# The entry of a two-block transformer kernel: modulation products shared between two engines, x normed by parts, two output groups run together

## The reference

```python
c_act = silu(c)                              # c: 2048 values
mod = c_act @ w_ada + b_ada                  # w_ada: 2048 x 12288
sh1, sc1, gt1, sh2, sc2, gt2 = split(mod, 6)
h = rmsnorm(x, g_mix) * (1 + sc1) + sh1
proj = h @ w_in                              # w_in: 2048 x 11344
q_a, k_a, v_a, q_b, k_b, v_b, qi, ki, wi, g_a, g_b = split(proj, ...)
...
x = x + (1 + gt1) * mixer(h, ...)
```

## Time and profile before

| | us |
|---|---|
| median of 3 runs (lowest, highest) | 2721.91 (2721.4, 2722.2) |
| the profiled execution's own time | 2720.93 |
| span of the profile, first to last instruction | 2719.1 |
| PE busy in the span | 2598.8 (96%) |
| DVE busy in the span | 1949.7 (72%) |
| ACT busy in the span | 1217.5 (45%) |

### The profile page before, as it was taken

One profiled execution on the slowest core, in us unless ns is written; L12 is line 12 of the kernel. 1 busy time (PEld: TensorE's weight loads), 2 busy tenths in 40 slices (PEclk: granted clock), 3 DMA queues, 4 the chain that ended last, 5 costly groups with the idle time before them and its releaser, 6 DMA issues.

```text
span 2719.1 us, 39494 instructions
## 1 busy us (share of the span) xinstructions
PE 2598.8 (96%) x14637; PEld 2265.9 (83%) x14637; DVE 1949.7 (72%) x2761; ACT 1217.5 (45%) x1578; POOL 101.5 (4%) x145
## 2 busy tenths in 40 slices
PE   3499999999999999999999999998999999999998
PEld 3388888888887888888888888886888888888887
DVE  6986778887788988855666656998776645566554
ACT  1244653444554655544555552003554443444443
POOL 0011111100001000000000000000000000000000
PEclk8599999999999999999999999999999999999999
DMA  8898677875678677755666554552556655666553
GB/s 312 308 291 274 210 241 241 252 213 155 218 249 269 209 248 248 242 186 188 187 190 187 190 166 141 154 155 78 192 180 187 191 187 191 188 187 191 186 186 132
DMA packets 492581, 557.33 MB, mean 205 GB/s; under 512 B 18855, under 2 KB 458280, under 8 KB 492200
## 3 DMA queue, kind: packets, MB, share of 16 engines
q1 hardware_dynamic: 474023, 488.50, 56.1%
q0 software_dynamic: 18432, 67.12, 8.2%
HBM read 553.45 MB, written 2.10 MB: 204 GB/s over the span
## 4 chain that ended last, share of the span: by engine, by line
PE 92%; DVE 4%; issue 2%; DMA 1%; ACT 1%; SPq 1%; POOL 0%; DVEq 0%; ACTq 0%
PE ps L1467 53%; PE ps L1469 26%; PE ps L1757 8%; DVE wlo L865 1%; PE ms L1520 1%; DVE norm_rows L962 1%; PE ms L1498 1%; DMA att<-in_w_ada 1%; PE ms L1782 1%; DMA att<-in_x 0%; PE ms L1611 0%; DVE tCDE L962 0%; SPq L396 0%; PE ms L1767 0%; PE ms L1545 0%
## 5 line engine op out<-in xcount | busy, mean ns | idle before, releaser
L865 DVE TENSOR_TENSOR wlo<-raw,whi 128x1024 fp32r<-128x1024 f32 x794 | 971.0, 1224 | 619.7 <-ACT whi L522 609.9
L1467 PE MATMUL ps<-xhl,whi 128*128 128x512 f32 x4352 | 1381.9, 399 | 23.0 <-DVE xhl L926 16.7
L522 ACT CAST whi<-raw 128x1024 fp32r<-128x1024 f32 x794 | 831.4, 1050 | 1126.6 <-PE ps L1469 1045.4
L1469 PEld LDWEIGHTS ps<-xhl,wlo 128*128 128x128 f32 x4352 | 821.0, 189 | 193.9
L1469 PE MATMUL ps<-xhl,wlo 128*128 128x256 f32 x4352 | 858.6, 279 | 0.0
L1467 PEld LDWEIGHTS ps<-xhl,whi 128*128 128x128 f32 x4352 | 666.8, 190 | 33.2 <-issue 32.7
L1467 PE MATMUL ps<-ghl,whi 128*128 128x512 f32 x1024 | 319.7, 393 | 0.0
L1469 PEld LDWEIGHTS ps<-ghl,wlo 128*128 128x128 f32 x1024 | 192.3, 188 | 44.3
L1757 PE MATMUL ps<-xg,raw 128*128 128x256 f32 x1024 | 221.3, 379 | 0.0
L1467 PE MATMUL ps<-fhl,whi 128*128 128x512 f32 x704 | 219.3, 393 | 0.0
L1757 PEld LDWEIGHTS ps<-xg,raw 128*128 128x128 f32 x1024 | 194.7, 190 | 26.2
(11 more groups left out here) (245 smaller groups left out, 1500.3 us busy)
## 6 DMA issues: line engine op xcount, KB each, us to landing
raw<-in_w_in SPq DMA_DIRECT2D x176, 512.0 KB, 4.3
raw<-in_w_up SPq DMA_DIRECT2D x176, 512.0 KB, 4.2
ada<-in_w_ada POOLq DMA_DIRECT2D x128, 512.0 KB, 4.7
raw<-in_ffn_w_up SPq DMA_DIRECT2D x128, 512.0 KB, 3.7
raw<-in_ffn_w_down SPq DMA_DIRECT2D x128, 512.0 KB, 3.4
raw<-in_conv_w_pw SPq DMA_DIRECT2D x96, 512.0 KB, 3.6
raw<-in_w_down SPq DMA_DIRECT2D x88, 512.0 KB, 3.3
att<-in_w_ada SPq DMA_DIRECT2D x32, 1024.0 KB, 7.3
```

The costliest lines, as they stand in the source:

```text
L522: nc.scalar.copy(whi[t % SPL][:, :, :], raw[t % RAW][:, :, :]).then_inc(s_hi, 1)
L865: nc.vector.tensor_tensor(wlo[t % SPL][:, :, :], raw[t % RAW][:, :, :], whi[t % SPL][:, :, :].bitcast(F32), ALU.subtract).then_inc(s_lo, 1)
L1467: mm(o[:, m, :, :], whi[t % SPL][:, c, m * P:(m + 1) * P], x, start=first and c == 0, stop=last and c == KC - 1, skip_group_check=True)
L1469: ins = mm(o[:, m, 0, :], wlo[t % SPL][:, c, m * P:(m + 1) * P], x[:, 0, :], start=False, stop=last and c == KC - 1, skip_group_check=True)
```

## The change

For the first eight modulation groups, which are now taken in the order 0, 4, 1, 5, 2, 6, 3, 7 (a shift group and its scale group make a pair, `FIRST`):

- Quarter 0 of K (`BY_TENSOR` = 4 chunks) is no longer multiplied by DVE. PE loads each 128x128 block of w_ada as weights and multiplies it by one column of `cact` (`first_columns`, 16 one-column products a group), into the same PSUM column to which `first_modulation` then adds DVE's two sums. This quarter has two buffers, the others one each.
- DVE makes the other 12 products and, between its first four and its last eight, other work (`beside`): reading out the group before, the root in group 2, norming four chunks of x in groups 2, 4 and 6 (`norm_first`), two wlo in groups 3, 5 and 7.
- Output groups 0 and 1 are multiplied together through K, as units 0 to 7 (`EARLY`): an even unit goes to `ps[0]`, an odd one to `ps[1]`, both with the same four chunks of x. A pair of units stands in groups 3, 5 and 7 between `first_columns` and `first_modulation`, the last pair after group 7. SP loads the pairs behind groups 1, 3, 5 and 6.
- `c` moves up in the list of vectors; SP loads the identity and the first 128 rows of vectors first, then w_ada and x, then the rest. ACT copies the two other blocks of vectors.
- The rotary angles and sines move out of the entry into `background` of steps 5 to 13.
- The main loop starts at t = 5 (unit 8), and the half pieces follow a new schedule (`pieces_by`): none in steps 0 to 2, two in steps 4, 7 and 10, otherwise one. POOL's first two are sent for at the end of the seventh group.

```diff
+BY_TENSOR = 4
+BY_VECTOR = DC - BY_TENSOR
+EARLY = 8
+B_ANGLE = 5
 
...
+def pieces_by(s):
+
+    return max(0, s - 2) + (s >= 4) + (s >= 7) + (s >= 10)
+
...
 
-VECS = [("b_ada", 96), ("g_mix", 16), ("g_ffn", 16), ("conv_b", 88), ("conv_w", 264), ("g_final", 16),
+VECS = [("b_ada", 96), ("c", 16), ("g_mix", 16), ("g_ffn", 16), ("conv_b", 88), ("conv_w", 264), ("g_final", 16),
         ("norm_mix_g_2", 16), ("norm_ffn_g_2", 16), ("final_norm_g_2", 16), ("conv_b_pw1_2", 32),
         ("conv_w_dw_2", 16 * TAPS), ("conv_b_dw_2", 16), ("conv_ln_g_2", 16), ("conv_ln_b_2", 16),
-        ("conv_b_pw2_2", 16), ("c", 16)]
+        ("conv_b_pw2_2", 16)]
 AT, _n = {}, 0
 for _name, _rows in VECS:
...
 
-        ada_first = [att[:, 32 + 8 * q:40 + 8 * q, :].rearrange("p (c m) t -> p c (m t)", c=4) for q in range(4)]
+        ada_first = [att[:, 32 + 8 * q:40 + 8 * q, :].rearrange("p (c m) t -> p c (m t)", c=4) for q in range(5)]
...
 
-        first_sum = [mod_sum, [tCDE[:, 0:NCOL], tCDE[:, NCOL:2 * NCOL]]]
...
+        first_vecs = [v for v in vec_parts if v[3] < P]
+        other_vecs = [v for v in vec_parts if v[3] >= P]
...
+            sp.dma_start(cons[:, 0:C_SW128], A["consts"][:, 0:C_SW128]).then_inc(s_in[0], 16)
+            load_vectors(sp, first_vecs, s_vin[0])
...
-            for q in range(4):
-                sp.dma_start(ada_first[q][:, :, :], w_ada[q][:, :, 0:NCOL]).then_inc(s_adaring[q], 16)
-            x_in = A["x"].rearrange("b (c p) (h t) -> p (b c) h t", p=P, t=T)
-            for c in range(2):
-                sp.dma_start(att[:, 8 * c:8 * c + 8, :], x_in[:, c]).then_inc(s_in[2], 16)
-            with sp.Fori(1, ADA_START) as g:
-                for q in range(4):
-                    sp.wait_ge(s_chain, g * DC + 4 * (q + 1))
-                    sp.dma_start(ada_first[q][:, :, :], w_ada[q][:, :, bass.ds(g * NCOL, NCOL)]).then_inc(s_adaring[q], 16)
+            def first_quarter(n, q):
+
+                cols_at = slice(FIRST[n] * NCOL, (FIRST[n] + 1) * NCOL)
+                if q == 0:
+                    if n >= 2:
+                        sp.wait_ge(s_firstmm, n - 1)
+                    sp.dma_start(ada_q0[n % 2][:, :, :], w_ada[0][:, :, cols_at]).then_inc(s_adaq0[n % 2], 16)
+                else:
+                    if n:
+                        sp.wait_ge(s_first, BY_VECTOR * (n - 1) + 4 * q)
+                    sp.dma_start(ada_first[q][:, :, :], w_ada[q][:, :, cols_at]).then_inc(s_adaring[q], 16)
...
-            columns(0, 28, w_in, 0)
+            for q in (1, 2, 3):
+                first_quarter(0, q)
+            x_in = A["x"].rearrange("b (c p) (h t) -> p (b c) h t", p=P, t=T)
+            for c in range(2):
+                sp.dma_start(att[:, 8 * c:8 * c + 8, :], x_in[:, c]).then_inc(s_in[2], 16)
+            first_quarter(0, 0)
+            sp.dma_start(posi, A["positions"]).then_inc(s_in[1], 16)
+            load_vectors(sp, other_vecs, s_vin[1])
+            sp.dma_start(cons[:, C_SW128:], A["consts"][:, C_SW128:]).then_inc(s_rest, 16)
+            for n in range(1, ADA_START):
+                for q in range(4):
+                    first_quarter(n, q)
+                if n in (1, 3, 5, 6):
+                    quad = {1: 0, 3: 1, 5: 2, 6: 3}[n]
+                    for k in range(2):
+                        load(0, 2 * quad + k, w_in[quad][:, :, CW * k:CW * (k + 1)])
+            columns(EARLY, 26, w_in, 2 * CW)
...
-                pool.wait_ge(s_chain, DC * (1 + ADA_START) + 2 * max(0, m - 1))
+                if m < 2:
+                    pool.wait_ge(s_first, BY_VECTOR * (ADA_START - 1))
+                else:
+                    pool.wait_ge(s_chain, DC * (1 + ADA_START) + 2 * (m - 1))
...
-            act.wait_ge(s_trc, 3)
+            act.wait_ge(s_trc, 1)
...
+                act.wait_ge(s_tr, 9 + b + 1)
+                lo = P + 4 * P * b
+                nc.scalar.copy(cols[:, lo:lo + 4 * P], (bank_z, bank_f)[(9 + b) % 2]).then_inc(s_trc, 1)
...
-            act.wait_ge(s_ang, 1)
-            for n in range(2):
-                nc.scalar.activation(rope[:, 2 * n, :], rB[:, T * n:T * (n + 1)], ACT.Sin).then_inc(s_sin, 1)
-                nc.scalar.activation(rope[:, 2 * n + 1, :], rA[:, T * n:T * (n + 1)], ACT.Sin).then_inc(s_sin, 1)
-            for t in range(SPL):
-                split_hi(0, t)
+            def first_hi(j):
+
+                for c in range(4 * j, 4 * j + 4):
+                    act.wait_ge(s_nt, c + 1)
+                    nc.scalar.activation(xh[:, c, :], sq[:, c % 4, :], ACT.Identity, bias=mod[:, c:c + 1]).then_inc(s_nh, 1)
+
             root(0)
-            norm_hi(0, lambda c: mod[:, c:c + 1])
+            for j in range(4):
+                first_hi(j)
+                split_hi(0, 2 * j)
+                split_hi(0, 2 * j + 1)
...
+                if s == B_ANGLE + 5:
+                    act.wait_ge(s_ang, 1)
...
-            for t in range(1, T_WAB + 1):
+            for t in range(EARLY - 3, T_WAB + 1):
                 split_hi(0, t + 3)
+                if t == EARLY - 1:
+                    low_out(0, 0, t)
...
+            def angles(step):
+
+                if step == 0:
+                    dve.wait_ge(s_posb, 1)
+                    dve.wait_ge(s_rest, 16)
+                    for n in range(2):
+                        sv.did(nc.vector.tensor_scalar(rA[:, T * n:T * (n + 1)], bank_o[:, T:2 * T], cons[:, C_FREQ + n:C_FREQ + n + 1], None, ALU.mult))
...
+                if step == 8:
+                    dve.wait_ge(s_sin, 4)
+                    for n in range(2):
...
+            def first_products(n, beside):
+
+                dve.wait_ge(s_gemv, n + 1)
+                for q in range(1, 4):
+                    dve.wait_ge(s_adaring[q], 16 * (n + 1))
+                    for c in range(4):
+                        i = 4 * (q - 1) + c
+                        sums, cx = first_sum[n % 2][i % 2], cact[:, 4 * q + c:4 * q + c + 1]
+                        w = ada_first[q][:, c, :]
+                        if i < 2:
+                            nc.vector.tensor_scalar(sums, w, cx, None, ALU.mult).then_inc(s_first, 1)
+                        else:
+                            dve.wait_ge(s_first, BY_VECTOR * n + i - 1)
+                            nc.vector.scalar_tensor_tensor(sums, w, cx, sums, ALU.mult, ALU.add).then_inc(s_first, 1)
+                    if q == 1:
+                        beside(n)
+
+            def read_first(n):
+
+                a = FIRST[n]
+                c = slice(4 * a, 4 * a + 4)
+                dve.wait_ge(s_gemv, 2 + n + 1)
+                nc.vector.tensor_tensor(mod[:, c], first_bank[n % 2][:, c], cols[:, AT["b_ada"] + 4 * a:AT["b_ada"] + 4 * a + 4], ALU.add).then_inc(s_firstmod, 1)
...
+            def norm_first(j):
+
+                c0 = 4 * j
+                dve.wait_ge(s_firstmod, 2 * j + 2)
+                sv.did(nc.vector.scalar_tensor_tensor(gmod[:, 0, c0:c0 + 4], mod[:, DC + c0:DC + c0 + 4], 1.0, cols[:, AT["g_mix"] + c0:AT["g_mix"] + c0 + 4],
+                                                      ALU.add, ALU.mult))
+                sv.wait()
+                if j:
+                    dve.wait_ge(s_h, c0)
+                for c in range(c0, c0 + 4):
+                    nc.vector.scalar_tensor_tensor(sq[:, c % 4, :], res[:, c, :], gmod[:, 0, c:c + 1], rstd[:, :], ALU.mult, ALU.mult).then_inc(s_nt, 1)
+                for c in range(c0, c0 + 4):
+                    dve.wait_ge(s_nt, c + 1)
+                    dve.wait_ge(s_nh, c + 1)
+                    nc.vector.scalar_tensor_tensor(xl[:, c, :], sq[:, c % 4, :], mod[:, c:c + 1], xh[:, c, :].bitcast(F32),
+                                                   ALU.add, ALU.subtract).then_inc(s_h, 1)
+
+            def beside(n):
+
+                if n:
+                    read_first(n - 1)
+                if n == 1:
+                    dve.wait_ge(s_in[1], 16)
+                    nc.vector.tensor_copy(posf, posi).then_inc(s_posf, 1)
+                if n == 2:
+                    root(0, EPS1, s_acc, 8)
+                if n in (2, 4, 6):
+                    norm_first(n // 2 - 1)
+                if n in (3, 5, 7):
+                    split_lo(0, n - 3)
+                    split_lo(0, n - 2)
...
-            with dve.Fori(0, ADA_START // 2) as i:
-                for par in range(2):
-                    dve.wait_ge(s_gemv, i * 2 + (par + 1))
-                    for q in range(4):
...
-            dve.wait_ge(s_sin, 4)
-            for n in range(2):
-                sv.did(nc.vector.tensor_scalar(rope[:, 2 * n + 1, :], rope[:, 2 * n + 1, :], cons[:, C_SIGN + n:C_SIGN + n + 1], None, ALU.mult))
-            read_modulation(0, ADA_START)
-            dve.wait_ge(s_mod, 1)
-            sv.did(nc.vector.scalar_tensor_tensor(gmod[:, 0, :], mod[:, DC:2 * DC], 1.0, cols[:, AT["g_mix"]:AT["g_mix"] + DC],
-                                                  ALU.add, ALU.mult))
-            for t in range(SPL):
```

(138 more changed lines are left out.)

101 lines of the change are left out of this document (37 added, 64 removed).

## The result

The changed kernel takes 2726.96 us (2723.7 to 2730.4, 19 runs) against 2721.91 (2720.2 to 2724.1, 19 runs) of the kernel before: ratio 1.0017, 95% interval 1.0011 to 1.0023. That is 5 us slower: small, within the 0.2% named above, but the interval lies clear of 1. Predicted was 2726. The profiled execution took 2724.95 us, its span is 2723.2 (before: 2720.93 and 2719.1). The 19 times of the changed kernel stand in two clumps, eight at 2723.7 to 2725.0 and eleven at 2726.9 to 2730.4, and the profiled one is among the eight.

What follows compares the result with a forecast made beforehand. Only the entry, the first 130 us, could give time back, with DVE and DMA equal bounds; PE's in-order chain then sets it. Unit 8 4.6 us later on 2720.93 gives 2725.5, the median 1.0 above: 2726, range 2708 to 2735.

Steps and rivals of the forecast that it cites:

- Columns by their count: PE in the entry: a group's 16 column products are 32 records, 7.1 us at half clock or 3.8 at full.
- The chain of two groups: Entry, from one even group's end on DVE to the next: PE's order makes it 30.3 us, before 20.1.
- The sign to look for: Timeline after: DVE's products wait for PE's sums in groups 4 and 6, for 5 us and more.
- First X: Entry: the first even-group end on DVE in the new chain, that of group 2, comes at 61 us.
- E: End of the entry's groups, with the last sums, those of group 7: 142.4 us.
- The tail: From the last sums to unit 8: reading, gain, scaling, wlo, units 6 and 7; 12.9 us, unit 8 at 155.3.
- yardstick: Start of unit 8 on PE, 150.70 us in the kernel before; forecast 4.6 us later.
- Pushed work at nothing: Behind the entry: 10.8 us of angles, rotary sign and half pieces moved onto DVE cost nothing.
- D: Rival, behind the entry: forecast entry, but pushed work starves PE, half its price 5 us, 2731 us; chance 0.08.
- B: Rival, entry: columns with units keep PE's clock up, unit 8 at 137, 13.4 us earlier, 2708 us; chance 0.17.
- C: Rival, entry: PE's clock never rises inside, last sums at 153.5, 2737 us; chance 0.08.
- What follows is the same PE work, back to back: From unit 8 on: PE's work is unchanged and without gaps, so unit 8's start measures the change.

Runs made afterwards that it cites:

- dup: Changed kernel with every column product of groups 2 to 7 issued twice, the second into an unused bank: 2757.33 us in one run.
- sums_first: Changed kernel with the odd group's sums ahead of its pair of units on PE's queue: 2719.72 us, 0.9990 of the kernel before.
- shift4: Changed kernel with 4 products that nobody reads between unit 7 and unit 8: 2727.12 us, 1.0015 of the kernel before.
- shift8: Changed kernel with 8 products that nobody reads between unit 7 and unit 8: 2730.78 us, 1.0030 of the kernel before.
- warm: Changed kernel with unread 256-column products behind each four column products and ahead of even groups' sums and units 6 and 7: 2737.48 us, 1.0056.
- units_last: Changed kernel with all eight units behind the sums of group 7, none inside the entry: 2729.13 us, 1.0022 of the kernel before.
- col2: Changed kernel with two chunks of each group as PE columns, not four, the other two on DVE: 2717.24 us, 0.9984 of the kernel before.
- col0: Changed kernel with no PE columns, all 16 products on DVE, quarter 0 last: 2719.36 us, 0.9991 of the kernel before.
- sums_col2: Changed kernel with odd groups' sums ahead of their units and only half the first quarter as columns: 2717.02 us, 0.9982 of the kernel before.
- sums_col2_keep: Changed kernel with odd sums ahead of units, half the columns, and 7 unread 256-column products before odd groups' sums: 2709.34 us, 0.9950 of before.

## Why the prediction was right, step by step

The mechanism was right, and that the time was only 1 us off is luck: unit 8 came 3.0 us earlier than forecast, the rest was 2.4 us longer, and the median lies 2.0 us above the profiled execution where 1.0 was added (to 2725.5, which gives 2726.5).

- **Columns by their count**, 7.1 us at half clock: 6.96 measured in four of the six groups of the chain, 5.24 and 6.00 in the two that began at full clock. The full-clock price of 3.8: 3.73 at 41.85 us. Right.
- **The chain of two groups**, 30.3 us: 28.9 and 28.1. The terms were a little high: sums and columns 10.3 for 10.7, the pair 7.7 and 7.0 for 7.9, reading to the next even group's end 9.0 for 9.8 with the handovers. That PE's order sets it is shown by dup (26.7 us for 28) and sums_first (2.5 us less a pair).
- **The sign to look for**, DVE waiting 5 us and more for PE in groups 4 and 6: 3.40 and 2.64 us. The chain was still PE's, but DVE had stood 2.92 and 2.94 us for a landing of w_ada just before, where I had put each sending condition 5 us and more ahead of DVE's need.
- **First X** 61: 61.7 here, but 64.8 and 67.2 in shift4 and shift8. I had taken the clock from 19 to 48 us as full, as before. In this profile it was not (the statistic took 9.49 us for 7.7), and an earlier x, from 17.97, made up for it. This term alone spreads over 5.5 us and was priced as a point.
- **E** 142.4: 139.0, from the chain. **The tail**, E + 12.9: E + 13.3. Unit 8: 152.28 for 155.3, so +1.6 for +4.6 on the yardstick. The chain, 3.4 us too long up to E, is the mis-sized term.
- **Pushed work at nothing**: the distance between the two kernels' PE was 1.67 us at 218 us and still at 378. Right. The rivals D, B and C did not happen: from unit 8 to 320 us PE has no idle time over 0.2 us but the 0.46 in front of that unit, and the clock came up in each pair of units (sums at 1.84) but not in the columns.
- **"What follows is the same PE work, back to back"**: the work is the same, its time was not, 2.4 us more in the profile. This step failed. I had read PE as nine tenths busy in every slice behind the first two, but the earlier trace rows has an 8 in the 28th, 1835 to 1903 us, where PE stands idle for 3.16, 2.43 and 6.27 us. Behind two of these gaps the clock fell in the change and not before. What the runs show is that falls of the clock behind such gaps come and go (shift4, shift8). Two profiles of the kernel before are without the two at the convolution and nine of eleven changed ones have them; whether the change makes them likelier, or nine of eleven is chance, stays open.
- **The median.** From the profiles the yardstick says +1.6, the rest +2.4, their sum 4.0 against 5.05 of the medians. The profiled execution read group 1 at 48.76, and five others of the same early code (sums_first, shift4, shift8, dup and warm) at 50.62 to 54.29, units_last at 48.23. The times fit: where DVE waits for PE at this read, they spread over 5.0 to 8.3 us (the change, sums_first, units_last, shift4, shift8; warm, with five runs, over 3.5), and where it doesn't, over 2.8 to 3.7 us (col2, col0, sums_col2, sums_col2_keep). That the other executions lose their microsecond there is still inferred; only profiles show the place.

Where the 22 us of units moved forward went is shown by units_last against the change: the way from the last sums to unit 8 is 11.0 us shorter (13.3 for 24.3) and the way to the last sums 10.9 longer, since the units stand between an odd group's columns and its sums, for which DVE waits. By sums_first the same units cost nothing there once the sums pass them: from reading group 1 to reading group 7 it takes 79.8 us, and units_last, with no unit inside, 80.0. And col2 against the change: 16 records of columns fewer a group gave 6.7 us.

## What to carry to other kernels

Work put into an engine's idle time is free only if nothing that another engine waits for is queued behind it: issue the short result first, then the long filling work. Count products by their records and at the clock that their own kind gets, not at that of their neighbours; in the entries of these runs the clock never rose in one-column products, and it fell in or right behind them, with and without gaps. Where an engine has to wait anyway, unread products of 256 columns just ahead of its next work paid here (one kernel, five runs), and among narrow ones they didn't. And where PE stands idle for some microseconds, don't take the time of the same work behind it as fixed to the microsecond.

## What was not expected of the hardware

- TensorE's clock fell in an unbroken stretch of work: with PE busy from 54 to 91 us in warm, eight column records took 1.24 us and the next eight 1.71. So idle time was not needed for the fall; what PE ran in it were one-column products and single fillers.
- Behind a gap of 3.15 to 3.16 us the same 62 records took 13.65 us in the kernel before and in shift4 and 15.34 in the change. Three such differences, of which one is in the change's favour, make up most of the 2.4 us by which the two profiles differ behind unit 8.
- Behind fourteen filler records the sums ran at full clock in all three odd groups of sums_col2_keep (6.11, 5.55 and 5.01 us of fillers, sums 1.87, 1.95 and 1.95).
